# A two-layer decoder trunk on one core: its input stage with x and the first weights loaded in halves, eight transpose banks, and casts and differences taken from PSUM

## The chip, the cores and the metric

The kernel runs on one core of a Trainium2 chip. The metric is the device time of one execution in microseconds (us), as the median of several runs. A profile, taken of one further execution, gives the durations and the waits that are read below. PE is TensorE, the matmul engine; DVE is VectorE; ACT is ScalarE; POOL is GpSimd; SP is the engine that only starts transfers. SBUF is the on-chip memory, PSUM the eight banks that PE writes into (`ps[:, 0..7, :]`, each 128 partitions x 512 floats).

## The reference, cut to what matters

```python
# x: (1, 512, 1024) f32; two layers; layer 0 is the DSA mixer, layer 1 the sliding-window one
h = rms_norm(x, attn_norm[0])            # x / sqrt(mean(x*x) + 1e-6) * gain
q_lat, c_kv, q_idx, k_idx, w_idx = _split(h @ a_w_in, [16*128, 128, 8*64, 64, 8])
score = sum_j w_idx[j] * relu(q_idx[j] . k_idx)     # the indexer: top 128 keys of each query
# softmax attention over the chosen keys with rel_bias[bucket(t - s)] added, then w_uv, w_out
x = x + mixer(h); x = x + swiglu(rms_norm(x, ffn_norm[0]))
# layer 1: the same with sliding-window attention and sinks; rms_norm at the end
```

## The kernel before

**Numbers in two parts.** Every float32 operand of a large product is split into a "hi" part (a cast to the float32r type) and a "lo" part (the value less hi). A product is three matmuls, hi x hi, lo x hi and hi x lo, on lines L549, L550 and L551, each 128 x 128 by 128 x 512. A tile of results, 128 output rows by 512 tokens over the eight 128-row blocks of the 1024 inputs, is 24 matmuls. x lies transposed in SBUF: `x[:, m, :]` is block m (128 of the 1024 features) of all 512 tokens.

**Weights** come as slabs (2 slots of `raw`, 1 MB each). SP starts the transfers in an order that is written out by hand (`slab(n)`), and slab n waits for `lo_done` of slab n-2, because it takes that slot. Then ACT casts it to `w_hi` in two halves (L973), and POOL subtracts to get `w_lo` (L440), again in two halves. PE waits for the half it needs. The first slab (number 0) is special: it holds the 72 columns of the index keys and index weights and the 128 columns of c_kv. Slabs 1 and 2 are the index queries. Slabs 3 to 10 are the latent queries.

**The input stage**, in the order of the work:

1. SP and ACT start the transfers: four pieces of `x_tok` (128 tokens x 1024 features, 512 KB each), two on either queue; the tables `tab` (identity, masks), the parameter rows, slab 0 (two transfers) and slab 1 (two).
2. PE transposes x: for each block m four 128 x 128 transposes (L610) into bank m % 4. From block 4 on a bank must first be read, so it waits for `x_new`.
3. DVE copies the bank to `x[:, m, :]` (L1355, `x_new`). ACT reads this copy, multiplies with the gain and casts to `xs_hi` (L1022). DVE takes the difference `xs_lo` (L1359), from x and xs_hi, both in SBUF. The copy of block m stands ahead of the difference of block m-1 on DVE.
4. PE makes the two small products for the table of position biases (L615, L616), DVE copies them (L1364, L1365, `g_done`), SP writes them to DRAM (`bias_row`), and one 4 MB transfer spreads them out (`bias_toep`, L362).
5. PE runs `first_tiles`: both tiles of slab 0 together, block by block (48 matmuls), after `x_new` of 6.
6. ACT squares the eight blocks of x into SBUF (`sq_first`, L1028), DVE adds them into `ss` (L1372). PE sums `ss` over partitions with a matrix of ones (`norm_sum`, L597), ACT takes the root (L1002), DVE the reciprocal (L1337), and DVE scales the first results (L1376, L1378 give `kw_done`, L1380 gives `craw_done`).
7. PE meanwhile does the two tiles of slab 1, then waits for `kw_done`, duplicates the index keys (L626), waits for `craw_done`, and does the two tiles of slab 2. The index scores follow (L558), then 16 rounds of top-8 selection on DVE, and everything after that.

[...]

## Time and profile before

| | |
|---|---|
| median of 3 runs | 1216.76 us (1216.35 to 1217.6) |
| the profiled execution's own time | 1218.91 us |
| its span, first to last instruction | 1217.1 us |
| busy in the span: PE, DVE, ACT, POOL | 96%, 49%, 38%, 48% |
| mean granted TensorE clock | 0.989 |

Times in the rows below count from the start of the span. The own time and the span differ by 1.8 us, which lie around the instructions. A matmul's row lasts longer than the step from one to the next, because matmuls overlap: a row of 0.39 us stands where they start every 0.23 us.

### The profile page before, as it was taken

To read this page: it belongs to the slowest core of one execution; us is meant where nothing else is said; L and a number is where in the kernel's file an instruction comes from. 1 tells how busy PE (TensorE), PEld (TensorE's weight loads), DVE (VectorE), ACT (ScalarE), POOL (GpSimd) and SP (SyncE) were. 2 spreads that over 40 slices of the span, in tenths; PEclk is the share of its full clock that TensorE was granted. 3 is DMA by queue.
4 is the path that set the end of the run, shared out by engine and by line. 5 is a ranking of instruction groups with operands and counts; after the bars stand their busy time and mean duration, and the time that the engine had idled before them with its cause. 6 is when DMAs were issued, how large, how long until landed. Compare 5 with 4: busy or idle time off the path is not lost.

```text
span 1217.1 us, 16258 instructions
## 1 busy us (share of the span) xinstructions
PE 1166.9 (96%) x5600; PEld 966.7 (79%) x5600; DVE 594.0 (49%) x1031; ACT 463.3 (38%) x857; POOL 581.3 (48%) x319
## 2 busy tenths in 40 slices
PE   5999999999999999999999989799999999999996
PEld 4767879988888888888888768688888888888885
DVE  5479877746644444432222489846634444321111
ACT  4252347763422233223222467633332223322222
POOL 4344847865444455444444554224444455434441
PEclk9999999999999999999999989899999999999998
DMA  5831411114333323323332542113233332323331
GB/s 167 240 104 35 138 36 53 44 44 127 82 103 103 98 80 97 103 72 95 95 95 61 153 104 53 36 36 103 72 102 103 103 90 83 92 78 93 91 94 69
DMA packets 178468, 110.42 MB, mean 91 GB/s; under 512 B 7180, under 2 KB 173127, under 8 KB 178424
## 3 DMA queue, kind: packets, MB, share of 16 engines
q1 hardware_dynamic: 177984, 108.69, 31.3%
q10 hardware_dynamic: 440, 1.17, 0.3%
q8 instruction: 25, 0.41, 0.1%
q14 instruction: 19, 0.16, 0.0%
HBM read 107.70 MB, written 6.33 MB: 94 GB/s over the span
## 4 chain that ended last, share of the span: by engine, by line
PE 83%; DVE 7%; issue 3%; DMA 2%; POOL 2%; ACT 2%; SPq 0%; ACTq 0%; DVEq 0%; POOLq 0%
PE ps L549 27%; PE ps L551 26%; PE ps L550 26%; POOL w_lo L440 1%; PE ps L755 1%; DMA b_toep<-bias_toep 1%; PE ps L558 1%; DVE work L1430 1%; DMA x_tok<-in_x 1%; DVE ss L1372 1%; DVE b_prob L1672 1%; PE ps L734 1%; DVE xs_lo L1359 1%; DVE work L1414 1%; DMA raw<-in_b_w_in 0%
## 5 line engine op out<-in xcount | busy, mean ns | idle before, releaser
L440 POOL TENSOR_TENSOR w_lo<-raw,w_hi 128x1024 fp32r<-128x1024 f32 (+1 forms) x200 | 463.0, 2337 | 509.7 <-ACT w_hi L973 501.1
L549 PE MATMUL ps<-xs_hi,w_hi 128*128 128x512 f32 (+3 forms) x1024 | 399.7, 390 | 9.1 <-DVE x L1355 3.7
L550 PE MATMUL ps<-xs_lo,w_hi 128*128 128x512 f32 (+3 forms) x1024 | 395.7, 386 | 0.0
L551 PE MATMUL ps<-xs_hi,w_lo 128*128 128x512 f32 (+3 forms) x1024 | 395.5, 386 | 0.0
L973 ACT CAST w_hi<-raw 128x1024 fp32r<-128x1024 f32 (+1 forms) x196 | 178.9, 962 | 435.0 <-PE ps L551 420.4
L549 PEld LDWEIGHTS ps<-xs_hi,w_hi 128*128 128x128 f32 x1024 | 193.1, 189 | 55.1 <-DVE x L1355 4.0
L550 PEld LDWEIGHTS ps<-xs_lo,w_hi 128*128 128x128 f32 x1024 | 193.0, 188 | 39.3 <-issue 1.1
L551 PEld LDWEIGHTS ps<-xs_hi,w_lo 128*128 128x128 f32 x1024 | 193.1, 189 | 38.9
L549 PE MATMUL ps<-act_hi,w_hi 128*128 128x512 f32 x352 | 139.2, 396 | 0.0
L551 PE MATMUL ps<-act_hi,w_lo 128*128 128x512 f32 x352 | 138.0, 392 | 0.0
L550 PE MATMUL ps<-act_lo,w_hi 128*128 128x512 f32 x352 | 136.6, 388 | 0.0
L1554 DVE TENSOR_TENSOR glu<-std,up 128x512 f32<-128x512 f32 x44 | 67.7, 1539 | 77.0 <-ACT std L1156 76.8
L1550 DVE TENSOR_TENSOR up<-ps,rstd 128x512 f32<-128x512 f32 x44 | 30.4, 692 | 138.6 <-PE ps L551 138.6
L1557 DVE TENSOR_TENSOR act_lo<-glu,act_hi 128x512 f32 (+1 forms) x44 | 76.3, 1734 | 41.5 <-ACT act_hi L1161 41.5
L1571 DVE TENSOR_TENSOR x<-ps,x 128x512 f32 x16 | 11.1, 692 | 175.0 <-PE ps L551 175.0
L551 PEld LDWEIGHTS ps<-act_hi,w_lo 128*128 128x128 f32 x352 | 66.1, 188 | 15.5
L550 PEld LDWEIGHTS ps<-act_lo,w_hi 128*128 128x128 f32 x352 | 66.1, 188 | 14.6
L549 PEld LDWEIGHTS ps<-act_hi,w_hi 128*128 128x128 f32 x352 | 66.2, 188 | 13.0
L1332 DVE TENSOR_TENSOR ss<-ss,sq_mem 128x512 f32<-128x512 f32 x32 | 55.2, 1725 | 9.8 <-ACT sq_mem L994 9.8
L1161 ACT CAST act_hi<-glu 128x512 f32 (+1 forms) x44 | 27.3, 621 | 76.9 <-DVE glu L1554 76.9
L1323 DVE SCALAR_TENSOR_TENSOR xs_lo<-x,params,xs_hi x24 | 25.1, 1046 | 52.3 <-ACT xs_hi L988 52.3
L495 POOL TENSOR_SCALAR prob<-prob,rinv 128x512 f32<-128x512 f32 (+3 forms) x32 | 34.1, 1084 | 13.7 <-DVE rinv L1503 13.7
(186 smaller groups left out, 1389.0 us busy)
## 6 DMA issues: line engine op xcount, KB each, us to landing
raw<-in_ffn_w_gate_up SPq DMA_DIRECT2D x88, 512.0 KB, 4.5
raw<-in_ffn_w_down SPq DMA_DIRECT2D x32, 384.0 KB, 3.6
raw<-in_a_w_in SPq DMA_DIRECT2D x21, 512.0 KB, 4.5
raw<-in_ffn_w_down SPq DMA_DIRECT2D x32, 320.0 KB, 4.0
raw<-in_b_w_in SPq DMA_DIRECT2D x10, 512.0 KB, 5.1
bias_toep<-bias_row SPq DMA_DIRECT2D x1, 4096.0 KB, 22.0
toep<-bias_toep SPq DMA_DIRECT2D x16, 256.0 KB, 2.6
raw<-in_a_w_out SPq DMA_DIRECT2D x8, 512.0 KB, 3.9
```

The source lines that it names most:

```text
L440: nc.gpsimd.tensor_tensor(pieces(w_lo, n)[half], pieces(raw, n)[half], pieces(w_hi, n)[half].bitcast(F32), ALU.subtract)\
L495: nc.gpsimd.tensor_scalar(at, at, rinv[:, par, i:i + 1], None, ALU.mult).then_inc(nrm_done, 1)
L549: nc.tensor.matmul(dst, wh, xh, start=start, stop=False, **kw)
L550: nc.tensor.matmul(dst, wh, xl, start=False, stop=False, **kw)
L551: return nc.tensor.matmul(dst, wl, xh, start=False, stop=stop, **kw)
L973: nc.scalar.copy(pieces(w_hi, n)[half], pieces(raw, n)[half]).then_inc(hi_done, 1)
L1161: nc.scalar.copy(act_hi[:, j + 2 * it, :], glu[:, j % 2, :]).then_inc(ah_done, 1)
L1323: nc.vector.scalar_tensor_tensor(xs_lo[:, bass.ds(m * T, T)], x[:, m, :], params[:, bass.ds(gain + m, 1)], xs_hi[:, bass.ds(m * T, T)].bit ...
L1332: nc.vector.tensor_tensor(ss[:, :], ss[:, :], sq[:, par, :], ALU.add).then_inc(ss_done, 1)
L1550: nc.vector.tensor_tensor(up[:, :], ps[:, b + 1, :], rstd[:, :], ALU.mult).then_inc(up_done, 1)
L1554: nc.vector.tensor_tensor(glu[:, v, :], silu[:, :], up[:, :], ALU.mult).then_inc(glu_done, 1)
L1557: nc.vector.tensor_tensor(act_lo[:, v + 2 * it, :], glu[:, v, :], act_hi[:, v + 2 * it, :].bitcast(F32), ALU.subtract)\
```

## The change

Eight things change, all in the first 40 us of the program or in the bias transfer:

- SP and ACT load x in two halves of its features (`x_part`: blocks 0 to 3, then 4 to 7, four transfers of 256 KB each) and slab 0 in two halves of its rows (`raw_part`). The identity comes first and alone; the rest of the tables comes later.
- PE transposes each block into a bank of its own (block m into bank m), so no block waits for `x_new`. Banks 6 and 7 hold the bias products between the two halves, and block 6 waits until DVE has copied them (`g_done`).
- ACT casts `xs_hi` straight from the bank, DVE takes the difference `xs_lo` from the bank, and the copy to `x` comes behind it.
- The bias products, and their copies on DVE, move in between the halves.
- `first_tiles` waits for `x_new` of 2. The first tile of slab 1 now stands ahead of `norm_sum`, only the second behind it.
- The squares go to three banks of PSUM in turn (4, 5 and 7) instead of `sq_first`, after all eight copies of x.
- ACT's cast of slab 2 (`split_after(0)`) stands ahead of the root; POOL's three mask subtractions stand behind slab 0.
- `bias_toep` is written by four transfers of 1 MB, each behind one weight slab, instead of one of 4 MB ahead of them.

```diff
+SQ_BANK = (4, 5, 7)
...
-            for t in (0, 2):
-                sp.dma_start(x_tok[:, t, :], x_in[0, t * P:(t + 1) * P, :]).then_inc(x_in_s, 16)
-            sp.dma_start(tab[:, :], consts[:, 0:C_HOT]).then_inc(tab_in, 16)
...
+            def x_part(half):
+
+                c = slice(half * T, (half + 1) * T)
+                for t in (0, 2):
+                    sp.dma_start(x_tok[:, t, c], x_in[0, t * P:(t + 1) * P, c]).then_inc(x_in_s[half], 16)
...
+                k = slice(half * DM // 2, (half + 1) * DM // 2)
+                sp.dma_start(r0[:, k, 0:DH + JI], aw[:, k, A_KI:A_KI + DH + JI]).then_inc(done, 16)
+                sp.dma_start(r0[:, k, P:2 * P], aw[:, k, A_CKV:A_CKV + R]).then_inc(done, 16)
...
-            sp.dma_start(bias_toep, skew).then_inc(toep_out, 16)
-            with sp.Fori(0, 4) as i:
-                for v in range(2):
-                    slab(S_A2 + v, i, wide(a_w_in[0], (2 * i + v) * 256))
-            sp.wait_ge(toep_out, 16)
+            for n in range(S_A2, S_AO):
+                slab(n, 0, wide(a_w_in[0], (n - S_A2) * 256))
+                if n < S_A2 + 4:
+                    h = 4 * (n - S_A2)
+                    skew = bass.AP(tensor=bias_row.tensor, offset=h * GLEN + P - 1, ap=[[GLEN, 4], [-1, P], [1, T]])
+                    sp.dma_start(bias_toep[h:h + 4], skew).then_inc(toep_out, 16)
+            sp.wait_ge(toep_out, 64)
...
+            def x_turn(half):
+
+                pe.wait_ge(x_in_s[half], 16 * NB)
+                for m in range(half * DM // 2, (half + 1) * DM // 2):
+                    if m == 6:
+
+                        pe.wait_ge(g_done, 2)
+                    for t in range(NB):
+                        last = nc.tensor.transpose(ps[:, m, t * P:(t + 1) * P],
+                                                   x_tok[:, t, m * P:(m + 1) * P], ident)
+                    last.then_inc(x_tr, 1)
...
-            pe.wait_ge(x_new, 6)
+            x_turn(1)
+
+            pe.wait_ge(x_new, 2)
             first_tiles((ps[:, 0, :], ps[:, 1, :]), 0, 0)
+
+            pe.wait_ge(x_new, 4)
+            tile(ps[:, 2, :], 1, 0, 0, 256, xh, xl)
             pe.wait_ge(set_up, 3)
             norm_sum(0)
-            tile(ps[:, 2, :], 1, 0, 0, 256, xh, xl)
             tile(ps[:, 3, :], 1, 0, P, 256, xh, xl)
...
             for m in range(DM):
-                act.wait_ge(x_new, m + 1)
-                nc.scalar.activation(xs_hi_m(m), x[:, m, :], ACT.Copy,
+                act.wait_ge(x_tr, m + 1)
+                nc.scalar.activation(xs_hi_m(m), ps[:, m, :], ACT.Copy,
                                      scale=params[:, GAIN[0] + m:GAIN[0] + m + 1]).then_inc(xhi_done, 1)
-                if m in (1, 3):
-                    split_half(0, m // 2)
+                if m in (1, 5):
+                    split_half(0, m // 4)
             split_hi(1)
             for m in range(DM):
-                nc.scalar.activation(sq_first[:, m, :], x[:, m, :], ACT.Square).then_inc(sq_done, 1)
+                act.wait_ge(x_new, DM if m < 3 else m + 1)
+                if m >= 3:
+
+                    act.wait_ge(ss_done, m - 2)
+                nc.scalar.activation(ps[:, SQ_BANK[m % 3], :], x[:, m, :], ACT.Square).then_inc(sq_done, 1)
+            split_after(0)
             norm(0)
-            split_after(0)
...
+            for m in range(DM):
+
+                dve.wait_ge(xhi_done, m + 1)
+                nc.vector.scalar_tensor_tensor(xs_lo[:, m * T:(m + 1) * T], ps[:, m, :],
+                                               params[:, GAIN[0] + m:GAIN[0] + m + 1],
+                                               xs_hi[:, m * T:(m + 1) * T].bitcast(F32),
+                                               ALU.mult, ALU.subtract).then_inc(xlo_done, 1)
+                nc.vector.tensor_copy(x[:, m, :], ps[:, m, :]).then_inc(x_new, 1)
+                if m == 1:
+
+                    dve.wait_ge(g_mm, 2)
+                    nc.vector.tensor_copy(g_sb[:, 0:T], ps[0:H, 6, :]).then_inc(g_done, 1)
+                    nc.vector.tensor_copy(g_sb[:, T:GLEN], ps[0:H, 7, 0:GLEN - T]).then_inc(g_done, 1)
...
-                nc.vector.tensor_tensor(ss[:, :], ss[:, :], sq_first[:, m, :], ALU.add).then_inc(ss_done, 1)
+                nc.vector.tensor_tensor(ss[:, :], ss[:, :], ps[:, SQ_BANK[m % 3], :], ALU.add).then_inc(ss_done, 1)
```

What moves on the engines is shown at three places. First PE, from its first transpose of x to its first matmul of slab 0. Before, all 32 transposes stand together, with four waits for `x_new`, and the bias products (L615, L616) behind them:

```order
L610 MATMUL ps<-tab,x_tok 128x128 [waits x_in]
L610 MATMUL ps<-tab,x_tok 128x128 x15
L610 MATMUL ps<-tab,x_tok 128x128 [waits x_new]
L610 MATMUL ps<-tab,x_tok 128x128 x3
L610 MATMUL ps<-tab,x_tok 128x128 [waits x_new]
L615 MATMUL ps<-hot,rel_sb 16x512 [waits rel_one,hot_in]
L616 MATMUL ps<-hot,rel_sb 16x128
L549 MATMUL ps<-xs_hi,w_hi 128x512 [waits xlo_done,lo_done,x_new]
```

Now, at the same place:

```order
L624 MATMUL ps<-tab,x_tok 128x128 [waits x_in_fore]
L624 MATMUL ps<-tab,x_tok 128x128 x15
L637 MATMUL ps<-hot,rel_sb 16x512 [waits par_done,rel_one,hot_in]
L638 MATMUL ps<-hot,rel_sb 16x128
L624 MATMUL ps<-tab,x_tok 128x128 [waits x_in_rear]
L624 MATMUL ps<-tab,x_tok 128x128 x7
L624 MATMUL ps<-tab,x_tok 128x128 [waits g_done]
L624 MATMUL ps<-tab,x_tok 128x128 x7
L566 MATMUL ps<-xs_hi,w_hi 128x512 [waits xlo_done,lo_done,x_new]
```

The four waits for `x_new` are gone; one for the second half of x and one for `g_done` stand in their place, and the bias products have moved between the halves.

Second DVE, from the parameters to the sums of the squares. Before, copy and difference alternate, with the bias copies (L1364, L1365) behind the last difference:

```order
L1348 COPY params<-ps 128x59 [waits par_t]
L1355 COPY x<-ps 128x512 [waits x_tr,par_done]
L1355 COPY x<-ps 128x512 [waits x_tr]
L1359 SCALAR_TENSOR_TENSOR xs_lo<-x,params,xs_hi 128x512 [waits xhi_done]
L1359 SCALAR_TENSOR_TENSOR xs_lo<-x,params,xs_hi 128x512 [waits xhi_done] x2
L1364 COPY g_sb<-ps 16x512 [waits g_mm]
L1365 COPY g_sb<-ps 16x128
L1372 TENSOR_TENSOR ss<-ss,sq_first 128x512 [waits sq_done,set_up]
L1372 TENSOR_TENSOR ss<-ss,sq_first 128x512 [waits ss_done,sq_done] x7
```

Now the difference comes first and reads the bank, and the bias copies stand after the second of eight pairs:

```order
L1383 COPY params<-ps 128x59 [waits par_t]
L1389 SCALAR_TENSOR_TENSOR xs_lo<-ps,params,xs_hi 128x512 [waits xhi_done,par_done]
L1393 COPY x<-ps 128x512
L1389 SCALAR_TENSOR_TENSOR xs_lo<-ps,params,xs_hi 128x512 [waits xhi_done]
L1397 COPY g_sb<-ps 16x512 [waits g_mm]
L1398 COPY g_sb<-ps 16x128
L1405 TENSOR_TENSOR ss<-ss,ps 128x512 [waits sq_done,set_up]
L1405 TENSOR_TENSOR ss<-ss,ps 128x512 [waits ss_done,sq_done] x7
```

The number of operations is the same; the operand that was `x` or `sq_first` in SBUF is now a bank of PSUM, and DVE waits for `g_mm` six pairs earlier.

Third SP, whose rows are the transfers that it starts, in order. Before, from the second row on:

```order
L348 DMA tab<-in_tables 128x640
L352 DMA raw<-in_a_w_in 128x8x72
L353 DMA raw<-in_a_w_in 128x8x128
L307 DMA raw<-in_a_w_in 128x4x256 x2
L357 DMA bias_row<-g_sb 16x640 [waits g_done]
L307 DMA raw<-in_a_w_in 128x4x256 [waits lo_done] x2
L359 DMA uv_raw<-in_a_w_uv 128x16x64
L362 DMA bias_toep<-bias_row 2048x1x512 [waits row_out]
```

Now, from the first row on, with the rows of the second half of x and of slab 0 read in the diff:

```order
L363 DMA tab<-in_tables 128x128
L355 DMA x_tok<-in_x 128x512 x2
L360 DMA raw<-in_a_w_in 128x4x72
L361 DMA raw<-in_a_w_in 128x4x128
L368 DMA tab<-in_tables 128x512
L309 DMA raw<-in_a_w_in 128x4x256 x2
L372 DMA bias_row<-g_sb 16x640 [waits g_done]
L374 DMA uv_raw<-in_a_w_uv 128x16x64
L309 DMA raw<-in_a_w_in 128x4x256 [waits lo_done,row_out]
L309 DMA raw<-in_a_w_in 128x4x256 [waits lo_done]
L381 DMA bias_toep<-bias_row 512x1x512
```

The first quarter of the table goes ahead of x, and slab 3 now stands ahead of the first quarter of the bias transfer instead of behind all of it.

## Rows read from the trace of the kernel before

**Rows 1.** Waits of PE in the whole run: us in total, times, longest.

```profile
PE ps L549 <- DVE x L1355: 3.7, 1, 3.7
PE ps L597 <- DVE ss L1372: 2.2, 1, 2.2
```

**Rows 2.** The chain that ended last, in order of time: start, us, what.

```profile
1.77 9.05 DMA x_tok<-in_x
...
14.39 0.60 DVE x L1355
...
15.65 0.60 DVE x L1355
...
48.75 1.05 PE ps L626 x2
```

**Rows 3.** Landings of x_tok; an issue in 0:4; a stretch (last: GB/s).

```profile
DMA to landing us min/median/max: 4.6/5.7/9.1
...
raw<-in_a_w_in SPq DMA_DIRECT2D x1, 512.0 KB, 10.8
...
5.00:8.00 3.00, 0.00 (x0) 0.00 (x0) 0.00 (x0) 0.00 (x0) 0.00 (x0) 1.00 1.03 413
```

**Rows 4.** Transposes by line (min/median/max ns), by stretch; timeline behind them.

```profile
L610 PE MATMUL ps<-tab,x_tok x32: 272/421/475, 10.9 to 16.7; 128*128 128x128 f32 x32
...
12.00:15.00 3.00, 3.00 (x16) 3.00 (x16) 2.75 (x5) 2.12 (x3) 0.00 (x0) 1.00 1.00 312
...
16.89 1.03 PE L615 MATMUL ps<-hot,rel_sb 33*16 33x512 f32 x2
...
17.76 0.38 PE L616 MATMUL ps<-hot,rel_sb 33*16 33x128 f32 x2
```

**Rows 5.** PE in order of time, 21 to 37.5: start, us, idle before.

```profile
21.82 0.80 PE L549 MATMUL ps<-xs_hi,w_hi 128*128 128x512 f32 x1 [3.68 <-DVE x L1355]
...
25.57 0.40 PE L549 MATMUL ps<-xs_hi,w_hi 128*128 128x512 f32 x1
...
34.20 0.39 PE L551 MATMUL ps<-xs_hi,w_lo 128*128 128x512 f32 x1
...
36.75 1.10 PE L597 MATMUL ps<-ss,ones 128*128 128x512 f32 x2 [2.16 <-DVE ss L1372]
```

**Rows 6.** ACT and DVE behind the sum over partitions, in order of time.

```profile
37.88 0.69 ACT L1002 ACTIVATE std<-ps,eps 128x512 f32<-128x512 f32 x1 [6.78 <-PE ps L597]
...
38.60 3.35 DVE L1337 RECIPROCAL rstd<-std 128x512 f32<-128x512 f32 x1 [2.00 <-ACT std L1002]
...
43.31 0.69 DVE L1378 COPY prob<-ps 8x512 f32<-8x512 f32 x1
```

**Rows 7.** Page groups (busy, mean ns), then single lines (min/median/max ns).

```profile
L1554 DVE TENSOR_TENSOR glu<-std,up 128x512 f32<-128x512 f32 x44 | 67.7, 1539 | 77.0 <-ACT std L1156 76.8
L1550 DVE TENSOR_TENSOR up<-ps,rstd 128x512 f32<-128x512 f32 x44 | 30.4, 692 | 138.6 <-PE ps L551 138.6
...
L1359 DVE SCALAR_TENSOR_TENSOR xs_lo<-x,params,xs_hi x8: 735/747/2246, 13.6 to 25.1; 128x512 fp32r<-128x512 f32 x8
...
L1028 ACT ACTIVATE sq_first<-x x8: 613/616/624, 26.8 to 30.5; 128x512 f32<-128x512 f32 x8
...
L1372 DVE TENSOR_TENSOR ss<-ss,sq_first x8: 691/692/2704, 27.6 to 35.9; 128x512 f32<-128x512 f32 x8
```

**Rows 8.** The difference L1359 beside POOL, in order of time.

```profile
15.33 2.53 POOL L440 TENSOR_TENSOR w_lo<-raw,w_hi 128x1024 fp32r<-128x1024 f32 x1 [4.27 <-ACT w_hi L973]
...
16.16 2.25 DVE L1359 SCALAR_TENSOR_TENSOR xs_lo<-x,params,xs_hi 128x512 fp32r<-128x512 f32 x1
```

**Rows 9.** ACT and POOL on slab 3, timeline; the page's DMA issues.

```profile
53.56 2.00 ACT L973 CAST w_hi<-raw 128x1024 fp32r<-128x1024 f32 x2 [2.16 <-DMA raw<-in_a_w_in]
...
54.70 4.75 POOL L440 TENSOR_TENSOR w_lo<-raw,w_hi 128x1024 fp32r<-128x1024 f32 x2 [10.36 <-ACT w_hi L973]
...
bias_toep<-bias_row SPq DMA_DIRECT2D x1, 4096.0 KB, 22.0
```

More of the change, by code:

```diff
@@ L231, in trunk @@
         unit_done = sem("unit_done")
-        tab_in, x_in_s, small_in, sink_in = sem("tab_in"), sem("x_in"), sem("small_in"), sem("sink_in")
+        id_in, tab_in, small_in, sink_in = sem("id_in"), sem("tab_in"), sem("small_in"), sem("sink_in")
+        x_in_s = [sem("x_in_fore"), sem("x_in_rear")]
+        raw_fore = sem("raw_fore")
         hot_in = sem("hot_in")
@@ L455, in _ @@
             nc.gpsimd.memset(work[:, :], 0.0).then_inc(set_up, 1)
-            pool.wait_ge(tab_in, TAB)
-            pool.wait_ge(set_up, 5)
-            for i in range(1, NB):
-                d = OFF[i] - P + i * P
-                nc.gpsimd.tensor_tensor(work[:, d:d + P], work[:, d:d + P], causal, ALU.subtract)\
-                    .then_inc(acc_zero, 1)
             for n in range(S_A2 + 2):
                 split_lo(n)
+                if n == 0:
+                    pool.wait_ge(tab_in, TAB)
+                    pool.wait_ge(set_up, 5)
+                    for i in range(1, NB):
+                        d = OFF[i] - P + i * P
+                        nc.gpsimd.tensor_tensor(work[:, d:d + P], work[:, d:d + P], causal, ALU.subtract)\
+                            .then_inc(acc_zero, 1)
             def q_part(h):
@@ L571, in tile, with first_tiles @@
                 last.then_inc(unit_done, 1)
-            def first_tiles(dst, n, e):
-                for k in range(DM):
+            def first_tiles(dst, n, e, ks=range(DM)):
+                for k in ks:
                     if k in (0, CUT_WIDE[0] // 256):
@@ L600, in _ @@
+            pe.wait_ge(id_in, 16)
             pe.wait_ge(small_in, 16)
             nc.tensor.transpose(ps[:, 7, 0:59], par_rows[:, :], ident[0:59, 0:59]).then_inc(par_t, 1)
-            for m in range(DM):
-                if m == 0:
-                    pe.wait_ge(x_in_s, 16 * NB)
-                if m >= 4:
-                    pe.wait_ge(x_new, m - 3)
-                for t in range(NB):
-                    last = nc.tensor.transpose(ps[:, m % 4, t * P:(t + 1) * P],
-                                               x_tok[:, t, m * P:(m + 1) * P], ident)
-                last.then_inc(x_tr, 1)
+            x_turn(0)
@@ L613, in _ @@
             pe.wait_ge(hot_in, 32)
             pe.wait_ge(rel_one, 1)
-            nc.tensor.matmul(ps[0:H, 5, :], rel_sb[:, :], hot[:, 0:T], start=True, stop=True).then_inc(g_mm, 1)
-            nc.tensor.matmul(ps[0:H, 4, 0:GLEN - T], rel_sb[:, :], hot[:, T:GLEN], start=True, stop=True).then_inc(g_mm, 1)
-            pe.wait_ge(x_new, 6)
+            pe.wait_ge(par_done, 1)
+            nc.tensor.matmul(ps[0:H, 6, :], rel_sb[:, :], hot[:, 0:T], start=True, stop=True).then_inc(g_mm, 1)
+            nc.tensor.matmul(ps[0:H, 7, 0:GLEN - T], rel_sb[:, :], hot[:, T:GLEN], start=True, stop=True).then_inc(g_mm, 1)
@@ L966, in split_half @@
             def split_half(n, half, it=0, after=0):
-                if half == 0:
+                if half == 0 and n == 0:
+                    act.wait_ge(raw_fore, 32)
+                elif half == 0 or n == 0:
                     act.wait_ge(raw_full[n % 2], 32 * (n // 2 + 1) + 32 * it)
@@ L1074, in _ @@
             nc.scalar.copy(uv_hi[:, :, :], uv_raw[:, :, :]).then_inc(uvh_done, 1)
[L1075 removed]
+            act.wait_ge(id_in, 16)
             nc.scalar.copy(ident_r[:, :], ident).then_inc(id_done, 1)
```

41 lines of the change are left out of this document (16 added, 25 removed).

## The prediction

> **What bounds the kernel now.** I read the page first: PE is busy for 96% of the span. A change helps only where PE waits, or where it sets free the chain in front of PE. The waits of PE name two in the stretch of the change: 3.7 us of a matmul of slab 0 for DVE's copies of x, and 2.2 us of the sum over partitions for DVE's sums [rows 1]. The chain that ended last runs, up to 49 us, through exactly these: the landing of the last piece of x at 10.8 us, DVE's copies and differences, the sums of squares, and then PE up to the duplication of the index keys (L626) at 48.75 [rows 2]. So every us taken from the way to L626 should come off the end, if what follows moves with it. The timeline of PE gives the stations: first matmul of slab 0 at 21.82, the last of its 48 at 34.20, the sum over partitions at 36.75 [rows 5]. The clock can be read there too. The first matmuls last 0.8 us, and 38 steps from 25.57 to 34.20 give 0.227 us each, which is the full clock of 2.4 GHz. 48 at full clock are 10.9 us, but the stretch took 12.6. The missing 1.7 us are matmuls at the lower clock of 1.2 GHz, after PE had stood idle for 3.68 us.
>
> **When the first matmul of slab 0 can start after the change.** It stands behind the second half of the transposes, and these (from block 6) behind `g_done`. I follow that chain.
>
> First, x. The four pieces of 512 KB land 4.6 to 9.1 us after their issue [rows 3]. The earliest is there at about 5.4, when roughly one piece on each of the two queues has moved, 1.0 MB. The first halves of x, the identity and the parameters ahead of them are 1.1 MB. At the 413 GB/s of the stretch 5 to 8 that is 5.7 us. The last piece of x took 9.1 us after its issue where the median was 5.7, so a late end is likely and I take 6.5. The bounds are 5.7, and 10.8, where all of x landed before [rows 2, 3].
>
> The Trainium skill speaks against small pieces: "DMA: Bandwidth & Descriptors", section "Measured", gives 341 GB/s for a transfer of 1 MB alone and 138 for 64 KB, and advises to batch to 1 MiB. An estimate from that page, at 200 GB/s, would put the first halves 3 us later, and the end 3 us later than my sum. The trace has 413 GB/s with several transfers of 512 KB in flight at once, and none of 256 KB.
>
> Sixteen transposes follow. At the lower clock a row lasts 421 ns and two overlap, and the stretch 12 to 15 holds 16 rows in 3 us [rows 4]: 0.21 each, 3.4 us. The bias products took 1.25 us, 16.89 to 18.14, at full clock [rows 4], so between 1.25 and 2.5; I take 2.2, nearer the low clock, since PE has only just begun. DVE's two bias copies are a step of 0.60 as for a copy of x [rows 2], and a shorter one: 0.9. By then blocks 4 and 5 are transposed. Blocks 6 and 7 are eight transposes at full clock, 272 ns a row in pairs [rows 4], 0.9 us, up to 1.7 if slow; hand-overs 0.3. The sum is 6.5 + 3.4 + 2.2 + 0.9 + 0.9 + 0.3 = 14.2. That is **7.6 us before 21.82**. The second half of x may land as late as 12 without moving this.
>
> **Does anything hold `first_tiles` then?** It takes 1.36 us a block (6 x 0.227), DVE needs 1.26 for a pair of copy and difference (14.39 to 15.65 [rows 2]). DVE has two blocks done before the bias copies end at 13.1, and the other six by 20.7; PE wants its last difference at 23.8. PE is the slower one throughout. Slab 0's second half landed at 13.6 before (2.82 + 10.8 [rows 3]) and is no later in the new order. Cast and POOL's subtraction, 2.5 us [rows 8], make it ready by about 17.5; PE wants it at 19.7. So the 48 matmuls run without a wait, and at full clock if PE has been at work since 6.5: **1.7 us** more.
>
> **Contention.** Before, the difference has a minimum of 735 ns and a maximum of 2246, and the sum of squares 691 and 2704 [rows 7]. The long ones stand beside POOL's subtraction, as at 16.16 [rows 8]. Two groups of the page with one shape say why: 44 operations with both inputs in SBUF average 1539 ns, 44 with one input in PSUM average 692, in one and the same loop, with POOL at work in it [rows 7]. After the change both kinds have one input in PSUM, so I count 0.66 us in a pair for the difference, and 0.80 a step for the sums.
>
> **The squares.** They start when all eight copies are there, 20.7, and ACT has had time to cast slab 1. ACT writes them into PSUM, which no row shows. To SBUF one costs 0.62 [rows 7]. Bounds: 0.5 and, with a long hand-over in the ring of three banks, 1.2 for a pair of square and sum. With 0.8 the sums end at 20.7 + 0.7 + 6.4 = 27.8; with 1.2 at 31. PE does slab 0 until 25.1 and the moved tile (24 x 0.227 = 5.5) until 30.6. At 0.8 the wait of **2.3 us** (34.43 to 36.75 [rows 5]) is gone; at 1.2 some 0.4 is left.
>
> **What is late next.** From the start of the sum over partitions to `kw_done` are 7.25 us: 36.75 to 44.00, through root, reciprocal of 3.35 and two scalings [rows 5, 6]. Two tiles (10.9 us) covered it. One is left: 1.1 + 5.5 = 6.6. So L626 waits **0.7 us**, which it did not before.
>
> ACT's cast of slab 2, now ahead of the root, has its condition (slab 0's products done) at 25.1 and is through by 27.5, long before 31.7: nothing. POOL's mask subtractions (1.3 us) move behind slab 0, and slab 1 is ready by 24, wanted at 25.1 and 27.8: nothing, with 1 to 4 us of cover. Slab 3 is wanted when slab 2's tiles end, at about 50.2. Before, it was cast at 53.56, two us after it could have been, since 4 MB of bias stood ahead of it [rows 9]. Now it stands ahead of them. POOL needs 4.75 and the cast 1.0, so it must have landed by 44. It is issued near 24 and has 20 us: nothing. The bias quarters need 22.0 / 4 = 5.5 us each [rows 9], and are read only after slab 10.
>
> **The sum.** 7.6 + 1.7 + 2.3 - 0.7 = 10.9 us. L626 starts at 37.8 instead of 48.75. Everything after it (index scores, top-8 rounds, attention) is started by results of PE, and by weights that wait for POOL, not by a fixed hour, so it moves as a block. Against the profiled execution's own 1218.91 that is 1208.0. The median of the runs lies 2.15 below this execution, so I predict 1216.76 - 10.9 = **1205.9 us**.
>
> **Rivals.**
>
> *x late or clock low, 0.19.* The first halves land up to 4.3 us later (10.8), or PE's gaps between its short jobs keep the clock low into slab 0, which cost 1.7 before. For: the last piece of x took 9.05 us [rows 2], and the two queues share the engines with slab 0's short rows. Against: half as many bytes are ahead. Gain 10.9 - 1.4 to 10.9 - 4.3, so 1207.3 to 1210.2.
>
> *The contention stays, 0.05.* If DVE waited for POOL with a PSUM operand too, five differences and two sums would take 1.5 and 2 us more each. Sums end at 39, PE waits 8.3 us for them. Gain 2.6: 1214.2. The 692 against 1539 speaks against it.
>
> *The gain is swallowed later, 0.05.* The stage of the top-8 rounds is bound by DVE; if it hung on something with an hour of its own, such as a weight slab, the end would not move: 1216.8, within 2.4. I find no such wait in the rows; DVE's accumulations start from PE's scores.
>
> *Slower, 0.04: slab 3 arrives by its old clock or later.* Place: PE's wait for `lo_done` before the index scores. If slab 3 shares the DMA engines with slab 2, uv and the first bias quarter, each us of landing past 44 costs one. At the old landing (53.5) the gain is down to about 1.4; past 54.9 the kernel is slower, for example 1219.5 at 58. That needs 31 us for 1 MB, where 22.0 sufficed for 4 MB [rows 9].
>
> *Faster still, 0.05.* x at 5.7, products at full clock, and one low-clock stretch less after 100 us: gain 13.5, 1203.3.
>
> **The numbers.** The forecast's own case, gain 9.4 to 12.4, has 0.62: 1204.4 to 1207.4. Range with the first rival and most of the last: 1203.2 to 1210.5, which leaves out about 0.15. A measurement of this kernel can tell about 0.2%, 2.4 us. Faster by more than that: 0.62 + 0.19 + 0.05 and most of the 0.05 of the contention, 0.90. Within: 0.06. Slower: 0.04.
>
> **What would show it.** First transposes near 6.5; first matmul of slab 0 near 14.2, and 0.23 us a step from there to 25; no difference over 0.8 us; sums of 0.69 us ending before 28 to 29; the sum over partitions right behind a matmul, near 30.6; L626 near 37.8 after a wait of 0.7; the cast of slab 3 near 41 with no wait for DMA. It would be wrong if x's first half lands past 9, if PSUM operands still wait for POOL, or if a wait on PE after 50 us grows by what was gained.

## The result and the profile after

The changed kernel takes 1208.63 us (median of 4 runs, 1207.13 to 1210.31) against 1216.61 us for the kernel before (1216.35 to 1217.6) beside it: a ratio of 0.993, 95% interval 0.9917 to 0.9942. It is faster, by 8.0 us of medians, where 10.9 were forecast. The profiled execution took 1209.77 us, span 1208.0, against 1218.91 and 1217.1: 9.1 us by profiles.

PE in order of time (start, us, idle before) in the changed kernel. L624 are the transposes, L637 and L638 the bias products, L566 to L568 the matmuls that were L549 to L551, L614 the sum over partitions, L652 the duplication of the index keys:

```profile
7.64 3.68 PE L624 MATMUL ps<-tab,x_tok 128*128 128x128 f32 x16 [2.53 <-DMA x_tok<-in_x]
11.24 1.89 PE L637 MATMUL ps<-hot,rel_sb 33*16 33x512 f32 x2
...
13.49 3.30 PE L624 MATMUL ps<-tab,x_tok 128*128 128x128 f32 x16
16.54 0.47 PE L566 MATMUL ps<-xs_hi,w_hi 128*128 128x512 f32 x1
...
32.76 0.39 PE L568 MATMUL ps<-xs_hi,w_lo 128*128 128x512 f32 x1
32.99 1.02 PE L614 MATMUL ps<-ss,ones 128*128 128x512 f32 x2
...
40.21 1.12 PE L652 MATMUL ps<-prob,tab 64*128 64x512 f32 x2 [0.71 <-DVE prob L1411]
```

Against [rows 5] the first matmul of slab 0 stands 5.28 us earlier (21.82 to 16.54), L614 3.76 us (36.75 to 32.99), since a tile of 5.5 us was put ahead of it, and L652 8.54 us (48.75 to 40.21, [rows 2]). L614 follows the matmul of 32.76 without a wait. From L652 to the end of the span are 1167.8 us, and 1168.4 before: what was won ahead of L652 came off the end.

DVE, POOL and ACT, the same view:

```profile
18.17 0.73 DVE L1389 SCALAR_TENSOR_TENSOR xs_lo<-ps,params,xs_hi 128x512 fp32r<-128x512 f32 x1
...
22.74 6.23 DVE L1405 TENSOR_TENSOR ss<-ss,ps 128x512 f32<-128x512 f32 x8 [0.74 <-ACT ps L1063]
```

```profile
17.19 2.40 POOL L456 TENSOR_TENSOR w_lo<-raw,w_hi 128x1024 fp32r<-128x1024 f32 x1 [2.99 <-ACT w_hi L1002]
...
20.80 4.79 POOL L456 TENSOR_TENSOR w_lo<-raw,w_hi 128x1024 fp32r<-128x1024 f32 x2
```

```profile
25.11 0.60 ACT L1063 ACTIVATE ps<-x 128x512 f32<-128x512 f32 x1 [0.19 <-DVE ss L1405]
...
42.80 2.02 ACT L1002 CAST w_hi<-raw 128x1024 fp32r<-128x1024 f32 x2
```

The difference at 18.17 runs inside POOL's subtraction of 17.19 and takes 0.73, where the one beside POOL took 2.25 before [rows 8]. The eight sums take 6.23 us though POOL works beside them until 25.6. Squares into PSUM take 0.60. The cast of slab 3 starts at 42.80 with no wait for DMA [rows 9].

The page of the changed kernel, busy time in the span:

```profile
PE 1165.8 (97%) x5600; PEld 965.4 (80%) x5600; DVE 587.2 (49%) x1031; ACT 463.0 (38%) x857; POOL 580.4 (48%) x319
```

### The profile page after: what moved, and what is told of

The parts are those of the page before. It is cut to its first block, busy times and chain, and to the rows that moved or that the text cites. A ratio compares the mean times of both kernels' runs of the same rounds, so it can differ in the third digit from the quotient of the medians.

```text
span 1208.0 us, 16227 instructions
## 1 busy us (share of the span) xinstructions
PE 1165.8 (97%) x5600; PEld 965.4 (80%) x5600; DVE 587.2 (49%) x1031; ACT 463.0 (38%) x857; POOL 580.4 (48%) x319
## 4 chain that ended last, share of the span: by engine, by line
PE 84%; DVE 7%; issue 3%; ACT 1%; DMA 1%; POOL 0%; DVEq 0%; ACTq 0%; SPq 0%
PE ps L566 27%; PE ps L568 27%; PE ps L567 27%; PE ps L781 1%; DVE b_prob L1705 1%; PE ps L575 1%; DVE work L1463 1%; DVE b_prob L1684 1%; PE ps L760 1%; DVE work L1447 1%; DVE bpt_lo L1350 1%; DMA raw<-in_b_w_in 1%; PE ps L908 0%; DVE b_rsum L1696 0%; DVE xs_lo L1350 0%
## 5 line engine op out<-in xcount | busy, mean ns | idle before, releaser
L566 PE MATMUL ps<-xs_hi,w_hi 128*128 128x512 f32 (+3 forms) x1024 | 398.9, 390 | 5.4 <-POOL w_lo L456 2.2
L568 PE MATMUL ps<-xs_hi,w_lo 128*128 128x512 f32 (+3 forms) x1024 | 395.2, 386 | 0.0
L566 PEld LDWEIGHTS ps<-xs_hi,w_hi 128*128 128x128 f32 x1024 | 192.7, 188 | 51.1 <-issue 3.4
L568 PEld LDWEIGHTS ps<-xs_hi,w_lo 128*128 128x128 f32 x1024 | 192.6, 188 | 38.7
L566 PE MATMUL ps<-act_hi,w_hi 128*128 128x512 f32 x352 | 139.2, 396 | 0.0
L568 PE MATMUL ps<-act_hi,w_lo 128*128 128x512 f32 x352 | 138.0, 392 | 0.0
L568 PEld LDWEIGHTS ps<-act_hi,w_lo 128*128 128x128 f32 x352 | 66.1, 188 | 15.5
L566 PEld LDWEIGHTS ps<-act_hi,w_hi 128*128 128x128 f32 x352 | 66.2, 188 | 13.0
```

The source lines that it names most:

```text
L566: nc.tensor.matmul(dst, wh, xh, start=start, stop=False, **kw)
L568: return nc.tensor.matmul(dst, wl, xh, start=False, stop=stop, **kw)
```

## The experiments

All are edits of the changed kernel. Each was timed in five rounds beside the kernel before, in three groups, each on one chip; before was at 1217.71 us (runs 1, 2, 3, 4), 1217.22 (5 to 8) and 1217.43 (9 to 12). "Station" is the start of the index keys' duplication in the profile of that kernel (L652; another line where the edit moved it).

| run | median us | ratio to before, 95% | first matmul of slab 0 | station |
|---|---|---|---|---|
| 1 unchanged | 1209.25 | 0.9924 [0.9910, 0.9938] | 17.09 | 40.74 |
| 2 warm-up | 1207.64 | 0.9913 [0.9900, 0.9927] | 14.83 | 38.49 |
| 3 bias products late | 1208.19 | 0.9923 [0.9909, 0.9936] | 14.09 | 38.15 |
| 4 both | 1209.08 | 0.9926 [0.9912, 0.9939] | 14.92 | 40.22 |
| 5 x whole | 1210.61 | 0.9947 [0.9933, 0.9960] | 16.29 | 39.96 |
| 6 sum first | 1210.81 | 0.9944 [0.9930, 0.9957] | 16.70 | 41.02 |
| 7 sum first, squares in SBUF | 1218.55 | 1.0007 [0.9998, 1.0016] | 16.43 | 49.54 |
| 8 difference from SBUF | 1212.31 | 0.9954 [0.9940, 0.9967] | 17.35 | 42.99 |
| 9 longer warm-up | 1205.41 | 0.9897 [0.9882, 0.9912] | 15.10 | 38.91 |
| 10 one bias transfer | 1209.5 | 0.9926 [0.9913, 0.9940] | 16.49 | 40.15 |
| 11 unchanged | 1207.69 | 0.9921 [0.9907, 0.9934] | 17.07 | 40.73 |
| 12 x whole | 1210.16 | 0.9947 [0.9933, 0.9960] | 16.36 | 39.99 |

The question of the first group: the first matmul of slab 0 came 2.3 us later than forecast. My theory was the low clock, the rival the bias products in PE's way.

**1, unchanged.** 

> The changed kernel once more, as the measure for the kernels beside it. Its first profile had the first matmul of slab 0 at 16.5 us, the duplication of the index keys (the station) at 40.2, and its four times fell into two pairs, near 1207.3 and near 1210.0. Theory A, the clock: the pairs differ by where the lower clock's stretches fall, so the station stays within 1.5 us of 40.2 and the mean granted clock goes down as the time goes up. Theory B, the transfers: the pairs differ by when x lands, so the station itself moves by up to 2.7 us with the landing. Median 1207 to 1210.

Measured 1209.25 (1206.0 to 1210.88), the first matmul at 17.09. Neither theory is borne out whole. The station moved by 0.5 us, with x 0.6 us later (8.24 against 7.64), which is less than theory B needs. But the mean granted clock does not follow the time, as theory A has it: it was 0.990 in the run of 1206.0 us, 0.993 in that of 1209.25 and 0.991 in that of 1210.88.

**2, warm-up.** 

> Six matmuls of no use (ones times zeros, into a bank that is written later) keep TensorE at work from about 1.5 to 7.3 us, before x lands at 7.6. Theory A: the 2.4 us that the first matmul of slab 0 came later than predicted are mostly the lower clock during transposes and bias products. Then the 16 first transposes take 1.8 us instead of 3.6, the products 1.2 instead of 2.2, the second half starts when x's rear lands (12.1), and the first matmul of slab 0 stands at 14.0 to 14.5 instead of 16.5, the station near 37.8, the time 2.4 us below the changed kernel, 1206.2. Theory B: the way is set by landings and by DVE's chain, not by the clock. Then the first matmul moves by less than 0.7 us and the time by less than 0.7.

```diff
+            pe.wait_ge(set_up, 3)
+            for _ in range(2):
+                nc.tensor.matmul(ps[:, 5, :], ones[:, :], ss[:, :], start=True, stop=True)
...
+            for _ in range(4):
+                nc.tensor.matmul(ps[:, 5, 0:P], ones[:, :], ss[:, 0:P], start=True, stop=True)
             x_turn(0)
```

PE in order of time, and its granted clock in two stretches (PEclk, before the last two columns; the page's 1.00 is 2.4 GHz, 0.50 is 1.2). The trace has no record of the clock ahead of its first rise, and this view shows 1.00 there too, as the row of 12 to 15 in [rows 4] does, where the transposes ran at the low clock until 15.0. So below, the first rise of a run is the start of its first record of full clock, and the rows' lengths agree with it.

```profile
5.37 1.16 PE L635 MATMUL ps<-ss,ones 128*128 128x128 f32 x8
8.24 3.48 PE L624 MATMUL ps<-tab,x_tok 128*128 128x128 f32 x16 [1.71 <-DMA x_tok<-in_x]
11.66 1.13 PE L642 MATMUL ps<-hot,rel_sb 33*16 33x512 f32 x2
...
12.94 2.13 PE L624 MATMUL ps<-tab,x_tok 128*128 128x128 f32 x16
14.83 0.47 PE L566 MATMUL ps<-xs_hi,w_hi 128*128 128x512 f32 x1
```

```profile
8.60:11.80 3.20, 3.20 (x16) 2.85 (x15) 1.72 (x3) 2.22 (x3) 0.00 (x0) 0.50 1.10 343
12.00:15.00 3.00, 3.00 (x21) 2.08 (x20) 2.64 (x6) 2.53 (x6) 2.37 (x1) 1.00 1.10 344
```

The products and the rear transposes now run at full clock (1.13 and 2.13 us, where the changed kernel shows 1.89 and 3.30), but the first sixteen transposes don't (3.48): the clock had fallen again (at 8.49), behind 1.71 us in which PE stood idle for x. The station is 2.25 us earlier, the median 1.6 us lower than run 1, though their single runs overlap (1206.65 to 1208.24, and 1206.0 to 1210.88).

**3, bias products behind slab 1's second tile, their transfers one slab later.** 

> The two bias products move from between the halves of x to behind the second tile of slab 1, DVE's copies of them behind the scaling of c_kv, and the bias transfers one slab later. Theory A: nothing but the landing of x's rear (12.1) and transposes at the lower clock (3.4 us) stands in front of slab 0: first matmul at 15.6, or near 14.0 if the clock rises earlier without the small products in between; the products then cost about 1.2 us behind the tile, of which 0.7 lie in the wait for the key scaling. Station 39.8 (low clock) or 38.2 (clock up), time 0.4 or 2.0 us below the changed kernel. Theory B, DVE's wait for the products is what delays the later differences: no gain at the first matmul, and the time 0.5 us above.

```diff
-                    if m == 6:
-                        pe.wait_ge(g_done, 2)
...
             tile(ps[:, 3, :], 1, 0, P, 256, xh, xl)
+            nc.tensor.matmul(ps[0:H, 5, :], rel_sb[:, :], hot[:, 0:T], start=True, stop=True).then_inc(g_mm, 1)
```

```profile
7.57 3.58 PE L623 MATMUL ps<-tab,x_tok 128*128 128x128 f32 x16 [2.75 <-DMA x_tok<-in_x]
12.08 1.94 PE L623 MATMUL ps<-tab,x_tok 128*128 128x128 f32 x16 [0.93 <-DMA x_tok<-in_x]
14.09 0.47 PE L568 MATMUL ps<-xs_hi,w_hi 128*128 128x512 f32 x1
```

The first matmul stands at 14.09: the rear transposes run at full clock and behind a wait for x. The products at 36.97 cost 0.4 us there: the index keys are ready at 37.70, and PE takes them up at 38.15. Most of their time lies in the 0.7 us that PE was to wait anyway. The station moves by 2.6 us, the median by 1.1.

**4, runs 2 and 3 together.** 

> Both edits together. Theory A: with the clock up the products are hidden behind DVE's first pairs and x's rear anyway, so moving them gains nothing on top: first matmul at 14.0, station 38.2, which is 0.5 us later than with the warm-up alone, for the products now stand behind the tile; time near 1206.6. Theory B (the products hold DVE and so the stage): 1 us or more below the warm-up alone.

The two do not add. The first transposes run at full clock (1.97), behind an idle time of 1.05 us. PE then stands idle for 2.32 us ahead of the rear half of x, and the clock is 0.50 from 14.14 to 17.55, in slab 0 itself:

```profile
8.55 1.97 PE L623 MATMUL ps<-tab,x_tok 128*128 128x128 f32 x16 [1.05 <-DMA x_tok<-in_x]
...
12.84 2.43 PE L623 MATMUL ps<-tab,x_tok 128*128 128x128 f32 x16 [2.32 <-DMA x_tok<-in_x]
```

```profile
14.20:17.40 3.20, 3.20 (x12) 2.70 (x11) 3.20 (x6) 2.67 (x4) 2.23 (x2) 0.50 0.63 199
```

The matmuls of slab 0 start 0.43 us apart there, where full clock gives 0.23. Most of what was won ahead of slab 0 is lost in it: the first matmul is 2.17 us earlier than in run 1, the station 0.52.

**5 and 12, x in four whole transfers.** 

> x goes back to four transfers of 512 KB, and both halves of the transposes wait for all four; everything else is as in the changed kernel. My theory: the halves are worth what they bring the first transposes forward. x lands near 10.8 instead of 7.6 to 8.2, the rear transposes need no wait, so the first matmul of slab 0 stands near 19.4 instead of 16.5 to 17.1, and the kernel is 2.5 to 3.3 us slower than the changed one: about 1211.5. Rival one: x in larger pieces lands nearly as early, because 256 KB pieces move slower; then the first transposes stand before 9.5 and the time is within 1 us of the changed kernel. Rival two: PE, starting later, gets its clock at the same time as before relative to the chip, so that the second sixteen transposes run at full clock and half of the loss is given back: 1 to 1.5 us slower only.

```diff
-                    sp.dma_start(x_tok[:, t, c], x_in[0, t * P:(t + 1) * P, c]).then_inc(x_in_s[half], 16)
+                    if half == 0:
+                        sp.dma_start(x_tok[:, t, :], x_in[0, t * P:(t + 1) * P, :]).then_inc(x_in_s[0], 16)
```

```profile
9.43 3.67 PE L625 MATMUL ps<-tab,x_tok 128*128 128x128 f32 x16 [4.92 <-DMA x_tok<-in_x]
...
14.40 2.13 PE L625 MATMUL ps<-tab,x_tok 128*128 128x128 f32 x16
16.29 0.47 PE L567 MATMUL ps<-xs_hi,w_hi 128*128 128x512 f32 x1
```

My main theory (x at 10.8, first matmul at 19.4) fell. All of x is there at 9.43, and the second sixteen transposes are at full clock, so the first matmul is no later than with halves: rival one had the landing (before 9.5), rival two the clock. Yet the median is 1210.61. Since the two disagree, I ran it once more beside the unchanged kernel:

> The kernel with x in four whole transfers once more, beside the changed kernel on one chip. Its first profile had the first matmul of slab 0 at 16.29, no later than with halves (16.54), since x landed whole at 9.4 and the clock rose before the rear transposes; but its median was 2 us above that of the changed kernel on another chip. Theory: the stations say that halves are worth nothing, and the medians of the two will lie within 0.8 us of each other. Rival: halves are worth about 2 us in most executions, and that one profile had an early landing; then the median is 1.5 us or more above the changed kernel's, and the profile shows x landed after 10.

> The changed kernel itself once more, on the same chip as the three others, as their yardstick. From the runs so far: 1208.6 to 1209.3 us, a ratio of 0.9925 to the kernel before, first matmul of slab 0 between 16.4 and 17.1.

Again the station is 0.7 us ahead of the unchanged kernel's (39.99 against 40.73), and again the median is 2.5 us behind it (1210.16 against 1207.69; 1209.68 to 1212.9, and 1207.24 to 1210.72). So halves are worth about 2 us in the timed runs, and nothing in the profiled executions. For the unchanged kernel the profiled execution is among the slowest of its runs each time (1209.77 of a median of 1208.63, 1210.88 of 1209.25, 1210.72 of 1207.69); with x whole it is among the fastest (1209.79 of 1210.61, 1210.08 of 1210.16). The rival's condition, x landed after 10, wasn't seen.

**6, both tiles of slab 1 behind the sum.** 

> Both slab 1 tiles stand behind the sum over partitions, as before the change. My theory: the moved tile hides the end of DVE's sums, but little is left to hide, since the sums end at 29.0 in the profile of the changed kernel and PE is through with slab 0 at 27.6. PE waits 1.3 to 1.6 us for the sums, the wait of 0.7 us of the index keys' duplication goes away, and that duplication stands 0.5 to 0.9 us later: the time is 0.5 to 0.9 us above the changed kernel. Rival: the forecast's term of 2.3 us for the moved sum is real, then the kernel is 1.6 us or more slower (2.3 less the 0.7). Second rival: PE's idle of 1.5 us lowers the clock, as in the run with the warm-up, and it loses 1 to 2 us more.

```diff
-            tile(ps[:, 2, :], 1, 0, 0, 256, xh, xl)
             pe.wait_ge(set_up, 3)
             norm_sum(0)
+            tile(ps[:, 2, :], 1, 0, 0, 256, xh, xl)
```

```profile
29.10 1.10 PE L614 MATMUL ps<-ss,ones 128*128 128x512 f32 x2 [1.25 <-DVE ss L1405]
...
41.02 1.12 PE L652 MATMUL ps<-prob,tab 64*128 64x512 f32 x2
```

A wait of 1.25 for the sums, none at L652, the station 0.81 later than in the first profile of the changed kernel, as my theory had it. The median is 1.6 to 3.1 us above those of runs 1 and 11, timed in other groups: more than the stations give, and not explained. (Its profiled execution has 2 us more behind the station; see the last section.) The clock did not fall behind this wait.

**7, run 6 with the squares in SBUF.** 

> As the run with both slab 1 tiles behind the sum over partitions, and ACT writes its squares to SBUF, so DVE's sums have two SBUF inputs. Set against that run it prices the squares in PSUM with nothing to hide them. Theory of contention: sums beside POOL's subtraction of slab 1 (20.8 to 25.6 us) take 2 to 2.7 us each and the rest 0.7, they end near 30.5 instead of 29, and the time is 1.0 to 2.0 us above the other run. Rival: squares in SBUF need no ring of three banks and no hand-over, so the steps without POOL go from 0.79 to 0.70, ACT runs ahead, and the two effects cancel: within 0.3 us. Second rival: POOL's subtractions are held up by DVE in turn and slab 1 comes too late; then PE waits for the difference of slab 1.

```diff
-                nc.scalar.activation(ps[:, SQ_BANK[m % 3], :], x[:, m, :], ACT.Square).then_inc(sq_done, 1)
+                nc.scalar.activation(sq_first[:, m, :], x[:, m, :], ACT.Square).then_inc(sq_done, 1)
```

DVE, POOL and PE, in order of time:

```profile
22.67 12.55 DVE L1403 TENSOR_TENSOR ss<-ss,sq_first 128x512 f32<-128x512 f32 x8 [0.77 <-ACT sq_first L1061]
...
20.72 5.23 POOL L457 TENSOR_TENSOR w_lo<-raw,w_hi 128x1024 fp32r<-128x1024 f32 x2
28.79 5.09 POOL L457 TENSOR_TENSOR w_lo<-raw,w_hi 128x1024 fp32r<-128x1024 f32 x2 [2.84 <-ACT w_hi L1003]
...
35.37 2.05 PE L615 MATMUL ps<-ss,ones 128*128 128x512 f32 x2 [7.79 <-DVE ss L1403]
```

The theory of contention had the mechanism, with 1 to 2 us where 7.7 were measured. The sums take 12.55 us instead of 6.23, up to 2.72 each, because they meet two slabs' subtractions and not one. PE waits 7.79 us, its clock falls to 0.50 from 29.8 to 40.0, and all of the change's gain is gone (1.0007), though x, the transposes and the differences are as in the changed kernel. The station is 8.52 us later than in run 6: 6.27 from the later start of the sum over partitions, the other 2.25 from the matmuls behind it at the low clock.

**8, the difference from x in SBUF.** 

> DVE copies a block of x first and takes the difference from x in SBUF (two SBUF inputs) instead of from PSUM. Theory of contention: the differences of the blocks that stand beside POOL's subtractions (17.2 to 25.6 us in the changed kernel) take near 2.2 us instead of 0.75, so DVE is through with x 4 to 6 us later, the sums end near 34 instead of 29, the sum over partitions waits 1 to 2 us, and the time is 1 to 3 us above the changed kernel. Rival: the length of a difference is set by its own two passes and not by POOL; then no difference is over 0.9 us, and the time is the same within 0.3 us. Second rival: the differences are contended but PE, being the slower one, hides it all: over 2 us in the rows, and no change of the time.

```diff
-                nc.vector.scalar_tensor_tensor(xs_lo[:, m * T:(m + 1) * T], ps[:, m, :],
+                nc.vector.tensor_copy(x[:, m, :], ps[:, m, :]).then_inc(x_new, 1)
+                dve.wait_ge(x_new, m + 1)
+                nc.vector.scalar_tensor_tensor(xs_lo[:, m * T:(m + 1) * T], x[:, m, :],
```

```profile
11.95 2.94 DVE L1391 SCALAR_TENSOR_TENSOR xs_lo<-x,params,xs_hi 128x512 fp32r<-128x512 f32 x1
...
16.31 2.29 DVE L1391 SCALAR_TENSOR_TENSOR xs_lo<-x,params,xs_hi 128x512 fp32r<-128x512 f32 x1
...
26.64 0.75 DVE L1391 SCALAR_TENSOR_TENSOR xs_lo<-x,params,xs_hi 128x512 fp32r<-128x512 f32 x1
```

```profile
11.43 1.15 PE L637 MATMUL ps<-hot,rel_sb 33*16 33x512 f32 x2
...
15.73 1.97 PE L624 MATMUL ps<-tab,x_tok 128*128 128x128 f32 x8 [1.91 <-DVE g_sb L1399]
...
26.06 0.50 PE L566 MATMUL ps<-xs_hi,w_hi 128*128 128x512 f32 x1 [1.06 <-DVE xs_lo L1391]
```

The four differences beside POOL's slab subtractions take 2.2 to 2.9 us, the other four 0.75. One of these (at 19.24) met a mask subtraction of POOL, and there it was POOL's operation that took 1.01 us, where the same one takes 0.47 in the changed kernel. Only the source, and with it the order of copy and difference, was changed. PE waits 1.91 us for the bias copies and 1.06 for a difference, and its clock is at 0.50 from 15.1 to 18.5. The station is 2.8 us later than in the first profile of the changed kernel.

**9, the warm-up up to x's landing** (ten of the small products instead of four). 

> The warm-up with ten instead of four useless products of 128 columns behind the parameters' transposition (these eight rows took 1.16 us, so twenty take near 2.9), which reach up to x's landing at 7.6 to 8.2 us. My theory: the clock fell at 8.49 in the first warm-up because PE stood idle for 1.7 us ahead of x. Without that idle time the first sixteen transposes take 2.0 instead of 3.5 us, the rear ones wait for the second half of x (12.0 to 12.4), and the first matmul of slab 0 stands near 14.2 instead of 14.83: 0.5 to 0.8 us below the first warm-up, about 2.2 us below the changed kernel. Rival one: the clock falls again anyway, before 15, in the gap of 0.5 to 1 us ahead of the rear half; then the time is that of the first warm-up or above it. Rival two: the filler reaches past x's landing and costs what it overhangs.

```profile
7.74 1.91 PE L624 MATMUL ps<-tab,x_tok 128*128 128x128 f32 x16
...
11.86 3.59 PE L624 MATMUL ps<-tab,x_tok 128*128 128x128 f32 x16 [1.03 <-DMA x_tok<-in_x]
```

```profile
12.10:15.30 3.20, 3.20 (x17) 3.20 (x16) 3.20 (x7) 2.74 (x5) 1.80 (x1) 0.50 1.09 347
```

The first transposes are fast (1.91), the rear ones slow (3.59): the clock fell behind an idle time of 1.03 us, as rival one said. By the station this is no better than run 2 (38.91 against 38.49). The median is the lowest of all, 1205.41 (4 runs, 1203.06 to 1207.08). Its profiled execution (1205.57) has 3 us less behind the station than the others, from the sliding-window stage near 705 us, so this median may owe as much to that stage as to the warm-up; see the last section.

**10, the bias in one 4 MB transfer.** 

> The skewed bias goes back to one transfer of 4 MB ahead of slabs 3 and later. It tests the forecast's rival on slab 3 and its price of nothing for the quarters. My theory: slab 3 now lands behind those 4 MB, near 20.6 + 2 + 22 + 3 = 48 instead of 31.5, so ACT's cast of slab 3 (42.80 in the changed kernel) waits about 5 us, POOL's subtraction ends near 54 instead of 48.7, and the first index scores, at 52.7 in the changed kernel, stand about 1.5 us later: the time 1.0 to 2.0 us above the changed kernel. Rival one: the scores do not need slab 3 before 54, the time is the same within 0.4 us. Rival two: all later slabs come late by one transfer as well and PE waits again for the next: more than 3 us slower.

```diff
+            skew = bass.AP(tensor=bias_row.tensor, offset=P - 1, ap=[[GLEN, H], [-1, P], [1, T]])
+            sp.dma_start(bias_toep, skew).then_inc(toep_out, 16)
             for n in range(S_A2, S_AO):
                 slab(n, 0, wide(a_w_in[0], (n - S_A2) * 256))
```

```profile
44.82 2.00 ACT L1000 CAST w_hi<-raw 128x1024 fp32r<-128x1024 f32 x2 [1.95 <-DMA raw<-in_a_w_in]
...
45.95 4.75 POOL L454 TENSOR_TENSOR w_lo<-raw,w_hi 128x1024 fp32r<-128x1024 f32 x2 [12.34 <-ACT w_hi L1000]
...
52.60 0.39 PE L573 MATMUL ps<-q_hi 64*128 64x256 f32 x2
```

The cast waits 1.95 us for slab 3, POOL is through at 50.7, and the scores, at 52.67 in the changed kernel, start at 52.60. The span is 1207.9, and 1208.0 there. By these rows rival one holds: the four quarters are worth nothing here, because PE has work until 52.4 and nearly 2 us of cover remain without them. The medians leave it less sure: 1209.5 against 1207.69 for the unchanged kernel in the same group, with single runs that overlap (1207.82 to 1209.73, and 1207.24 to 1210.72).

## Why the prediction came out as it did

The time is inside the range, and the gain was 2 to 3 us smaller than forecast. By its steps:

- **x in 6.5 us:** the first transposes stand at 7.64 (8.24 and 7.98 in runs 1 and 11), so this term was off by 1.1 us. I took 413 GB/s from pieces of 512 KB [rows 3]. From 5 to 8 us the changed kernel moves 354, which for 1.1 MB makes 0.4 us (an estimate). More was lost ahead of that: from 3 to 5 us it moves 211, where the kernel before moved 399 and run 5, with whole pieces, 370 (both stretches below). That is 0.3 to 0.4 MB less, near 1 us (an estimate), and the prediction took the start as it was before. The rule on small pieces that the prediction weighed, of the Trainium skill's "DMA: Bandwidth & Descriptors", section "Measured", had the right direction; the 3 us that the prediction worked out with it were too many.
- **From there to the first matmul:** the transposes take 3.6 (forecast 3.4), the products 2.25 (2.2), and the sixteen rear transposes 3.05, where I had 0.9 for the copies, 0.9 for blocks 6 and 7 at full clock and 0.3: 2.1. This is the other step that failed, by 0.95. The clock had not risen by 14, as that step needed, but at 16.3. (Two smaller readings: eight rows of 272 ns in pairs make 1.1 us and not 0.9, and sixteen transposes at the low clock take 3.60 us from the first to what follows, 0.225 each, where half of a row's 421 ns gave 0.21.) Together: 1.1 + 0.2 + 0.05 + 0.95 = 2.3, which is 16.54 less 14.2. Runs 2 and 3 give it back, with the first matmul at 14.83 and 14.09.
- **The low clock in slab 0, 1.7:** right. The 48 matmuls take 11.0 us where they took 12.6, with the clock up from 16.3 and no wait between them.
- **Contention:** right, and run 8 shows it with one edit: 0.73 from PSUM, 2.2 to 2.9 from SBUF beside POOL. The Trainium skill's "SBUF — State Buffer", section "Who interferes with whom", says that DVE and GpSimd share a port pair under an exclusive lock; the lengths of run 8 beside and without POOL agree (2.2 to 2.9 against 0.75).
- **Squares into PSUM, 0.8 a step:** 0.79. I named the wait of 2.3 us as what they remove. Run 7 shows that they can carry more: with SBUF squares and the sum first, PE waits 7.79 us, where with PSUM squares it waits 1.25 (run 6). The forecast compared with the sums of before (9.04 us, which met one slab's subtraction) and didn't ask what the earlier start would run them into. No run has SBUF squares with the moved tile; from run 7 an estimate is that the sums would end at 35.2, 2.2 us behind the tile (32.99).
- **The moved tile:** the wait of 2.3 is gone. With PSUM squares it hides only 1.25 us (run 6), and costs 0.71 at L652: forecast 0.7.
- **Slab 3, no wait for DMA:** right, and cheaper than I thought: the old single transfer would have served too, by the rows of run 10. The slower rival took its price from a landing at 53.5, which the new order doesn't come near even with 4 MB ahead (44.8). Its example is off by 0.4: 14 us past 44 make 1219.9 and not 1219.5.
- **Everything behind L652 moves as a block:** right within 0.6 us.

The parts add up: 5.28 + 1.6 + 2.3 - 0.7 = 8.5, the measured shift of the station. Of the likeliest rival, "x late or clock low", both mechanisms happened in part; the clock was low ahead of slab 0, not in it.

DMA in the stretches 3 to 5 and 5 to 8 us (last column GB/s), the changed kernel, then run 5:

```profile
3.00:5.00 2.00, 0.22 (x1) 0.18 (x1) 0.00 (x0) 0.62 (x1) 0.00 (x0) 1.00 0.92 211
5.00:8.00 3.00, 0.47 (x3) 0.36 (x3) 0.22 (x1) 0.86 (x2) 0.00 (x0) 1.00 1.10 354
```

```profile
3.00:5.00 2.00, 0.33 (x1) 0.18 (x1) 0.22 (x1) 1.49 (x2) 0.00 (x0) 1.00 0.95 370
5.00:8.00 3.00, 0.00 (x0) 0.00 (x0) 0.00 (x0) 0.00 (x0) 0.00 (x0) 1.00 1.01 406
```

What stays open: the profiled executions of the changed kernel are not typical of its runs, which reach from 1206.0 to 1210.9 in 14 executions. A rise of the clock near 11.7 in some of them, as run 8 shows it (below), would give about 2.3 us (an estimate from run 2, where the clock rose at 11.9: from the first transpose to the first matmul of slab 0 are 6.59 us there, and 8.90 in the changed kernel). The meeting of DVE and POOL near 705 us, which run 9 escaped (below), is worth 3. No profile caught the unchanged kernel in either. So the value of the halves, 2 us by medians and none by profiles, stays open too, and part of run 6.

## What to carry to other kernels

Ask of an operation that starts earlier what it now runs beside: here the sums, moved 5 us forward, would have met two of POOL's subtractions (run 7), and with a PSUM operand they took 6.23 us beside POOL all the same. Where PE starts cold behind a load, useless products can raise its clock ahead of the first matmul (runs 2 and 9: at 14.83 and 15.10, against 16.54 to 17.09), but look at each idle time behind them. The low clock came back behind idle times of 1.71 us (run 2), 2.32 (run 4), 1.91 (run 8) and 1.03 (run 9), and did not behind 0.93 (run 3), 1.05 (run 4) and 1.25 (run 6). Look for the same meeting elsewhere: PE's longest wait behind the input stage, 5.44 us near 713, has it as its cause. And price a transfer by a row with pieces of its size; if there is none, keep both ends in the range.
